# A two-layer mixing network followed by a transformer block, on one core: queue orders changed in the index, scan, attention and mixing stages

## The reference

```python
h = rms_norm(x, norm1_g[l]) * (1.0 + sc1) + sh1
proj = h @ w_in[l]
q, k, v, iq, ik, iw, z, xbc, dt_raw, ga, gm = jnp.split(proj, SPLIT_POINTS, axis=-1)
# q, k: normed and rotated; iq, ik: rotated
score = einsum("bqh,bqhs->bqs", iw, relu(einsum("bqhd,bsd->bqhs", iq, ik))) * IDX_SCALE
# 64 best keys of each query, softmax attention over them
o_attn = dsa_attention(q, k, v, iq, ik, iw, n_keep) @ w_attn_o[l]
xbc = silu(causal_dwconv(xbc, ssm_conv_w[l], ssm_conv_b[l]))   # 4 taps
y = ssd_scan(xs * dt_g, a_dt, bm, cm)       # decay = exp(cs[t] - cs[s]), s <= t, 32 heads
y = rms_norm((y + xs * d_skip) * silu(z), ssm_norm_g[l])       # by 4 groups
o_ssm = y @ w_ssm_o[l]
mixed = (sigmoid(ga) * o_attn + sigmoid(gm) * o_ssm) @ w_out[l]
x = x + g1 * mixed
h = rms_norm(x, norm2_g[l]) * (1.0 + sc2) + sh2
val, gate = jnp.split(causal_dwconv(h @ w_up[l], ffn_conv_w[l], ffn_conv_b[l]), 2, axis=-1)
x = x + g2 * ((silu(gate) * val) @ w_down[l])
```

## Time and profile before

| | |
|---|---|
| median of 3 runs | 1947.29 us (1946.86 to 1948.07) |
| profiled execution | 1950.46 us, span of its instructions 1948.8 us |
| PE busy | 1725.1 us, 89% of the span |
| POOL, DVE, ACT busy | 1165.8, 1005.3, 863.5 us |
| mean granted TensorE clock | 0.924 of full |
| read from HBM | 299.5 MB, 154 GB/s over the span |

### The profile page before, as it was taken

One profiled execution on the slowest core, in us unless ns is written; L12 is line 12 of the kernel. 1 busy time (PEld: TensorE's weight loads), 2 busy tenths in 40 slices (PEclk: granted clock), 3 DMA queues, 4 the chain that ended last, 5 costly groups with the idle time before them and its releaser, 6 DMA issues.

```text
span 1948.8 us, 33455 instructions
## 1 busy us (share of the span) xinstructions
PE 1725.1 (89%) x13290; PEld 1660.3 (85%) x13290; DVE 1005.3 (52%) x1772; ACT 863.5 (44%) x1411; POOL 1165.8 (60%) x476
## 2 busy tenths in 40 slices
PE   8978998979888999778999888888999895769999
PEld 8978988869888999778988778887999894669999
DVE  3457666456325886557666536424882247334400
ACT  2244444544335663244444454334664442324532
POOL 1346954545365889456865454455888683036886
PEclk8788999989899999888999998899999998578999
DMA  7334743436343558444754355444665652024664
GB/s 261 101 115 152 251 139 130 141 130 225 109 143 126 184 196 286 132 120 135 246 175 137 119 163 163 153 129 119 183 185 179 209 174 87 1 80 137 184 184 131
DMA packets 85513, 302.71 MB, mean 155 GB/s; under 512 B 9840, under 2 KB 12528, under 8 KB 85104
## 3 DMA queue, kind: packets, MB, share of 16 engines
q1 hardware_dynamic: 85360, 300.59, 48.3%
HBM read 299.50 MB, written 1.05 MB: 154 GB/s over the span
## 4 chain that ended last, share of the span: by engine, by line
PE 71%; DVE 15%; ACT 4%; issue 4%; DVEq 3%; DMA 1%; POOL 1%; SPq 0%; ACTq 0%; POOLq 0%
PE gemm_bank L1426 58%; PE turn_bank L1533 2%; DVE ada_acc L735 2%; ACT w_hi L404 2%; PE turn_bank L1503 1%; DVE conv L735 1%; PE outp_bank L1521 1%; PE score_bank L1426 1%; PE score_bank L1503 1%; DMA ada_w<-in_w_ada 1%; POOL w_lo L386 1%; DVE rstd_row L755 1%; DVE idx_score L735 1%; DVE probs L922 1%; PE outp_bank L1568 1%
## 5 line engine op out<-in xcount | busy, mean ns | idle before, releaser
L386 POOL TENSOR_TENSOR w_lo<-w_raw,w_hi 128x1024 fp32r<-128x1024 f32 x472 | 1165.6, 2476 | 771.4 <-ACT w_hi L404 770.9
L404 ACT ACTIVATE w_hi<-w_raw 128x1024 fp32r<-128x1024 f32 x472 | 492.3, 1046 | 767.2 <-PE gemm_bank L1426 738.0
L1426 PE MATMUL gemm_bank<-h_hi,w_hi 128*128 128x256 f32 x2112 | 617.8, 293 | 79.2 <-DVE h_lo L735 28.9
L1426 PE MATMUL gemm_bank<-h_lo,w_hi 128*128 128x256 f32 x2112 | 609.2, 288 | 0.0
L1426 PE MATMUL gemm_bank<-h_hi,w_lo 128*128 128x256 f32 x2112 | 608.6, 288 | 0.0
L1426 PEld LDWEIGHTS gemm_bank<-h_hi,w_hi 128*128 128x128 f32 x2112 | 417.8, 198 | 88.2 <-DVE h_lo L735 30.1
L1426 PEld LDWEIGHTS gemm_bank<-h_lo,w_hi 128*128 128x128 f32 x2112 | 417.8, 198 | 0.1
L1426 PEld LDWEIGHTS gemm_bank<-h_hi,w_lo 128*128 128x128 f32 x2112 | 417.2, 198 | 0.0
L1426 PE MATMUL gemm_bank<-w_hi,h_hi 128*128 128x256 f32 (+2 forms) x704 | 207.2, 294 | 18.4 <-DVE h_lo L735 8.0
L735 DVE SCALAR_TENSOR_TENSOR conv<-gemm_bank,params_sb,conv 128x255 f32<-128x255 f32 (+1 forms) x320 | 139.5, 477 | 140.7 <-ACT conv L567 69.8
L1426 PE MATMUL gemm_bank<-w_lo,h_hi 128*128 128x256 f32 (+2 forms) x704 | 202.7, 288 | 0.0
(11 more groups left out here) (276 smaller groups left out, 2407.4 us busy)
## 6 DMA issues: line engine op xcount, KB each, us to landing
w_raw<-in_stream SPq DMA_DIRECT2D x458, 512.0 KB, 3.6
ada_w<-in_w_ada SPq DMA_DIRECT2D x80, 512.0 KB, 4.7
ada_first<-in_w_ada SPq DMA_DIRECT2D x16, 512.0 KB, 10.5
w_raw<-in_stream SPq DMA_DIRECT2D x8, 256.0 KB, 2.7
alibi_sb<-in_alibi SPq DMA_DIRECT2D x1, 1920.0 KB, 7.2
rows_sb<-in_rows SPq DMA_DIRECT2D x1, 1536.0 KB, 10.5
residual<-in_x_t SPq DMA_DIRECT2D x1, 1024.0 KB, 7.4
out_x<-residual SPq DMA_DIRECT2D x4, 256.0 KB, 4.4
```

What stands on the lines that cost most here:

```text
L386: nc.gpsimd.tensor_tensor(w_lo[:, s, 0:n], w_raw[:, s, 0:n], w_hi[:, s, 0:n].bitcast(f32), ALU.subtract).then_inc(lo_ready, 1)
L404: A(w_hi[:, s, 0:n], w_raw[:, s, 0:n], ACT.Copy).then_inc(hi_ready, 1)
L1426: ins = M(o, a, b, start=first and i == 0, stop=last and i == len(passes) - 1, skip_group_check=True)
```

## The change

It does these things, in both layers if nothing else is said.

1. Index turns: DVE copies rounds 0 and 1 right behind the taps of unit 0, ahead of the softplus, and round 2 behind the taps of unit 1.
2. Index scores: ACT takes relu in place in PSUM and signals `relu_done`; DVE reads the bank and gives it back (`S.read`). The buffer `idx_relu` is no longer used.
3. Exponents: `pick` and `cs_split` have 128 rows in place of 64, the new ones zero.
4. Scan order on PE: the chunk of head h ahead of the exponents of head h+1.
5. End of the scan: on ACT the roots of the second half two parts into the tail rather than behind it; on DVE the low parts of the first half ahead of the scales of the second.
6. Last attention pair: `so_part(14)` ahead of the pair's values and transposes.
7. Mixing on ACT: the high parts between the weight copies of `U_AO` rather than behind them.
8. Modulation tiles of layer 0: eight in the up stage, on every other unit, and eight in the down stage, in place of sixteen there.

```diff
-        cs_split = sb("cs_split", [64, SEQ], f32r)
-        pick = sb("pick", [64, 32], f32r)
+        cs_split = sb("cs_split", [P, SEQ], f32r)
+        pick = sb("pick", [P, 32], f32r)
...
             if l + 1 < DEPTH:
-                slots += [((U_DN + i // 4, i % 4), ada_tile(l, "down", i)) for i in range(16)]
+                slots += [((U_UP + 2 * i + 2, 0), ada_tile(l, "down", i)) for i in range(8)]
+                slots += [((U_DN + i // 3, 2 * (i % 3)), ada_tile(l, "down", 8 + i)) for i in range(8)]
...
                             act.wait_ge(S.full[b], k + 1)
-                            if h >= 2:
-                                act.wait_ge(relu_used, l * IDX_HEADS + h - 1)
-                            A(idx_relu[:, h % 2, :], S.bank[b][:, 0:CW], ACT.Relu).then_inc(S.read[b], 1)
+                            A(S.bank[b][:, 0:CW], S.bank[b][:, 0:CW], ACT.Relu).then_inc(relu_done, 1)
...
-                late_parts(tail_parts(0, 5))
+                late_parts(tail_parts(0, 2))
                 y_roots(1)
+                late_parts(tail_parts(2, 5))
                 y_high(l, 0)
...
-                ahead(l, crossed(U_AO) + parts(U_AO + 2, U_OUT))
-                for j in range(4):
+                def mix_high(j):
                     act.wait_ge(mix_ready, l * 4 + j + 1)
                     A(HH[:, 2 * j:2 * j + 2, :], gates[:, 0, 2 * j:2 * j + 2, :], ACT.Copy, scale=0.5).then_inc(mix_hi, 1)
+                ahead(l, crossed(U_AO) + [(U_AO + 2, 0)])
+                mix_high(0)
+                mix_high(1)
+                ahead(l, [(U_AO + 2, 1), (U_AO + 3, 0)])
+                mix_high(2)
+                ahead(l, [(U_AO + 3, 1)])
+                mix_high(3)
...
-            V.tensor_tensor(pick[:], ident[0:64, 0:32], ident[0:64, 32:64], ALU.add)
+            V.tensor_tensor(pick[:], ident[:, 0:32], ident[:, 32:64], ALU.add)
+            V.tensor_scalar(cs_split[64:P, 0:P], ident[64:P, :], 0.0, None, ALU.mult)
+            V.tensor_scalar(cs_split[64:P, P:SEQ], ident[64:P, :], 0.0, None, ALU.mult)
...
                         b, k = S.use(l, S_IDX + h)
-                        dve.wait_ge(S.read[b], k + 1)
+                        dve.wait_ge(relu_done, l * IDX_HEADS + h + 1)
...
-                                ins = stt(idx_score[:, a:e], idx_relu[:, h % 2, a:e], iw[:, tt, h:h + 1], idx_score[:, a:e],
+                                ins = stt(idx_score[:, a:e], S.bank[b][:, a:e], iw[:, tt, h:h + 1], idx_score[:, a:e],
                                           ALU.mult, ALU.add)
-                        ins.then_inc(relu_used, 1)
+                        ins.then_inc(S.read[b], 1)
...
                     conv_taps(i)
+                    if i < 2:
+                        idx_turned((0, 1) if i == 0 else (2,))
                     if i == 0:
...
-                    elif i == 1:
-                        idx_turned()
                     elif 3 <= i < 7:
                         idx_scores(i - 3)
...
+                for f in range(8):
+                    y_low(f)
                 for f in range(8, 16):
                     y_scale(f)
-                for f in range(8):
-                    y_low(f)
...
                         up_low(i - 2)
+                    if l + 1 < DEPTH and i % 2 == 0 and 2 <= i < 18:
+                        ada(ada_tile(l, "down", i // 2 - 1))
...
-                        for i in range(4 * j, 4 * j + 4):
-                            ada(ada_tile(l, "down", i))
+                        for i in range(3 * j, min(3 * j + 3, 8)):
+                            ada(ada_tile(l, "down", 8 + i))
...
-                    if l < DEPTH and p < 7:
+                    if l < DEPTH:
                         so_part(2 * p)
...
                 if l < DEPTH:
-                    so_part(14)
                     so_part(15)
...
-                    row = pick[:, h:h + 1].to_broadcast([64, P])
+                    row = pick[:, h:h + 1].to_broadcast([P, P])
...
                 for h in range(16):
+                    part(l, *scan_part(h), token_chunk, HH, HL)
                     decay_exponents(h + 1)
-                    part(l, *scan_part(h), token_chunk, HH, HL)
...
                 for h in range(16, 32):
+                    late_part(*scan_part(h))
                     if h < 31:
                         decay_exponents(h + 1)
-                    late_part(*scan_part(h))
```

More of the change, by code:

```diff
@@ L254, in build @@
             sem("sq_ready"), sem("x_root"), sem("h_scaled"), sem("h_hi_ready"), sem("h_ready"))
-        idx_rot, relu_used = sem("idx_rot"), sem("relu_used")
+        idx_rot, relu_done = sem("idx_rot"), sem("relu_done")
         qk_squared, qk_sum, qk_root, q_rot, k_rot = sem("qk_squared"), sem("qk_sum"), sem("qk_root"), sem("q_rot"), sem("k_rot")
@@ L1038, in conv_taps, with idx_turned @@
                     ins.then_inc(gemm_read[b], 1)
-                def idx_turned():
-                    for r in range(3):
+                def idx_turned(rounds):
+                    for r in rounds:
                         b, k = T.use(l, T_IQ + r)
@@ L1049, in idx_scores @@
                         b, k = S.use(l, S_IDX + h)
-                        dve.wait_ge(S.read[b], k + 1)
+                        dve.wait_ge(relu_done, l * IDX_HEADS + h + 1)
                         for a, e, tt in ((0, P, 0), (P, CW, 1)):
                             if h == 0:
-                                ins = V.tensor_scalar(idx_score[:, a:e], idx_relu[:, 0, a:e], iw[:, tt, 0:1], None, ALU.mult)
+                                ins = V.tensor_scalar(idx_score[:, a:e], S.bank[b][:, a:e], iw[:, tt, 0:1], None, ALU.mult)
                             else:
-                                ins = stt(idx_score[:, a:e], idx_relu[:, h % 2, a:e], iw[:, tt, h:h + 1], idx_score[:, a:e],
+                                ins = stt(idx_score[:, a:e], S.bank[b][:, a:e], iw[:, tt, h:h + 1], idx_score[:, a:e],
                                           ALU.mult, ALU.add)
-                        ins.then_inc(relu_used, 1)
+                        ins.then_inc(S.read[b], 1)
                         dve.drain()
```

## The result

Before 1947.68 us (median of four runs, 1946.86 to 1949.45), changed 1928.18 us (four runs, 1925.02 to 1931.36), ratio 0.9905 with a 95% interval of 0.9885 to 0.9924. The profiled execution took 1931.36 us, its span is 1929.7 us; before it was 1948.8. Two of the four executions took 1931.3 us and two 1925.0, at a mean granted clock of 0.916 and 0.921, and the profiled one is of the longer pair. The change is faster, by 19.5 us where 55 were forecast.

A forecast was written before the change was run, and what follows sets the result against it. It took the kernel as bound by PE (71% of the chain; DVE 15%), with PE's waits for DVE left to win. Gains of 77.4 less 22 give 55.4, so a median of 1892 us; 8-in-10 range 1866 to 1924.

The forecast's parts named there:

- index stage: Turned queries copied earlier, score banks handed back by DVE: new PE stops and restarts, a loss of 11 per layer, -22 us.
- end of the scan: Root earlier on ACT, scales behind the first eight subtractions on DVE: 10.5 us saved per layer, +21.
- exponents: In the scan, 128 rows in place of 64 save 0.2 us for each of 62 heads, +12.4 us.
- order in the scan: Chunk ahead of the next head's exponents, so PE no longer waits there for DVE's `probs`: +9 us.
- last pair and mixing: Two terms: `so_part(14)` moved into PE's wait for `probsT`, +13 us; ACT's high parts made earlier at the mixing, +15.
- modulation tiles: Eight of layer 0's tiles moved into the up stage, relieving the down stage: +7 us.
- DVE's list up to the `ikT` copy is as long as before: Index stage: `ikT` is ready at 109.1 plus some 0.4 for the copy, leaving PE a wait of 5.2 us.
- 9.4 us leave the path: Scan's end: the root comes at about 407 and the scales stand behind eight subtractions, shortening DVE's chain by 9.4 us.
- a modulation tile sits between: Scan: where a tile (1.3 us or more) precedes the pair product, its exponents are late; 4 us given back.
- POOL holds up DVE: Rival, 14%: DVE waits for POOL at the scan's end, mixing, up-stage tiles and scan gates; 22 us (6 + 5 + 5 + 6) lost, 1914.
- The half clock throughout the index stage: Rival, 17%: the clock stays low between index stops of 6.2 us, 25 us more in two layers, 1917.
- The hand-over is free: Rival, 4%: the scores come early enough after all, 33.4 us shrinks to 7.6 per layer, 1840.

The follow-up runs named there:

- experiment 3: The changed kernel with the exponents over 64 rows again and no zero rows: 1940.52 us, 12.3 slower than the changed kernel.
- experiment 7: The changed kernel with the scan's end as before (root behind all five late chunks, scalings ahead of the low parts): 1938.67 us, 10.5 slower than the changed kernel.
- experiment 8: The changed kernel with the last attention pair and the mixing back in the old order: 1946.36 us, 18.2 slower than the changed kernel.
- experiment 4: The changed kernel with all sixteen modulation tiles in the down stage of layer 0 again: 1932.67 us, 4.5 slower, not clear of noise.
- experiment 5: The changed kernel with POOL's subtraction cut to 8 columns at thirteen chunks per layer: 1897.84 us, 30 us less than the changed kernel.
- experiment 10: The changed kernel with only heads 0 to 15 of the scan back in the old order: 1945.57 us, 17.4 slower than the changed kernel.
- experiment 6: The changed kernel with only heads 16 to 31 of the scan back in the old order: 1918.63 us, 9.6 us less than the changed kernel.
- experiment 2: The changed kernel with DVE's scores one unit earlier, relu still in PSUM: 1876.14 us, 52 us less than the changed kernel.

## Why the prediction was wrong

Faster was right; 1928.2 lies above the range of 1866 to 1924. By the landmarks the terms come to some 16.5 us in place of 55.4; the start and the end of the program make up the rest of the 19.1 between the two profiles. Of the 39 that are missing 15.5 belong to the index stage, which by itself put the time outside the range, and about 8 each to the end of the scan and to the last pair with the mixing.

| term | forecast | measured | by |
|---|---|---|---|
| index stage | -22 | -37.5 | landmarks |
| exponents | +12.4 | +12.3 | experiment 3 |
| order in the scan | +9 | +6 | both halves +18.5, less the exponents |
| end of the scan | +21 | +10.5 to 12.9 | experiment 7, landmarks |
| last pair and mixing | +28 | +18 to 20 | experiment 8, landmarks |
| modulation tiles | +7 | +2.7 to 4.5, not clear of noise | landmarks, experiment 4 |

*Index stage.* The mechanism was right, and its sign: six stops of 6.5 to 6.9 where 6.2 were forecast. The step that failed is "DVE's list up to the `ikT` copy is as long as before". It has the same instructions, but 3.7 us more. PE no longer stands still during softplus, so POOL goes on, and four of its steps are held up where two were; the stop was 8.6 for 5.2, and 1.7 at most in experiment 5. Nor did the sum hold the stop for `c_dot_b`, 2.8 per layer where it was 0.6, and 1.4 behind it (7.16 us for the next pair of chunks). By the rows it comes from DVE's running sum meeting POOL (scan and cast 2.4 us each, where before they took 0.7 and 0.3); no run takes these subtractions away. With 1.2 for the three longer stops, and 0.4 less of restarts, this is the 7.8 per layer.

*End of the scan.* "9.4 us leave the path" took the reciprocal and its steps at the durations of the earlier trace rows and left out that POOL stood still there only because PE did. Moved ahead of the stop, they run beside it and take 5.6 us more; experiment 7 shows the same steps short, experiment 5 shows them short in the new place without POOL. There the stage is 2.7 us shorter, in each layer, and ACT's high part, which the prediction named as next, sets the stop of 2.6 that is left. So POOL took 2.7 of the 4 us per layer that are missing. In the rest is PE's new wait of 1.0 to 1.2 us at the modulation sum; no run separates it.

*Exponents.* That 12.3 met 12.4 is in part luck: the price was 0.28 per head and not 0.2, and 5 us of it were hidden. Experiment 10 shows that the gain exists only in the new order.

*Scan.* The size of +9 was near, for a wrong reason. In layer 0 the first half, to the eighth pair product, gains 10.0 us and the second loses 0.7; in layer 1 they gain 7.0 and 2.2. In the second half "a modulation tile sits between" was not the trouble, but that the new order gathers two stops into one of 7.8, behind which more work runs at the low level (experiment 6). Undoing that half alone gains 9.6.

*Mixing and last pair.* Of the forecast 7.5 and 6.5 per layer 6.0 and 5.4 came in layer 0: 1.75 of stop is left at the mixing, and it is two subtractions held up; in experiment 5 the stop is gone and the stage 3.5 us shorter. In layer 1 the stage of the last pair gained only 2.8. The stops in it are no longer than in experiment 10, where it gained 7.2: the 4.4 between them is work at the low level (mean granted clock 0.91 for 0.99). What brings the clock down there stays open.

*Tiles.* "DVE has 25 us to give" was right, but each tile's sum except the first took 3.25 us or more beside POOL and PE waited 0.75 seven times.

*The rivals.* "POOL holds up DVE" was what happened, given 14%, and sized too small: 22 us at four places. Experiment 5, which leaves the tiles of the up stage alone, found 30, and in its trace half of the gain lies in the index stage, at softplus, which was not among the four. The half clock throughout the index stage did not come: restarts cost 9.2 of the forecast 9.6 per layer. "The hand-over is free" did not come either, but experiment 2 shows that it was one line away. The pair product did not wait in every pair.

*The signs named.* `idx_score` six times and some 37: 39.3. `ikT` twice and 10: 17.5, wrong. The line of 27.5 to fall to 6 to 8: 10.7. The mixing's stops to vanish: 1.75 each. `probs` near 3: the stops in front of the exponents went, and 23.5 stands at the pair product instead. Up and down stage within 6 us of layer 1: 189.4 us against the 178.8 of the earlier trace rows, wrong.

## What to carry to other kernels

A duration read from a stretch in which GpSimd stands still doesn't hold for the same instruction moved into a busy stretch: here 0.2 to 0.7 us became 2.1 to 2.9, and work of 9.4 us that was pulled out of a stop took 5.6 us more in its new place, 2.7 of them on PE's path. It also holds for work that isn't moved: end a stop of PE, and POOL goes on beside what stayed (softplus). When a resource is handed back by another engine than before, lay the two queues side by side and ask what stands ahead of the hand-back; one unit's shift was worth 52 us. In the second half of the scan one stop of 7.8 us cost more than two of 1.9 and 2.6, by 9.6 us in two layers, partly through the work at the low clock behind it.

## What was not expected of the hardware

- Operations with one SBUF input are held up as well: TENSOR_SCALAR 2.49 us for 0.43, CAST 2.42 for 0.28, and a TENSOR_SCALAR on 64 columns 1.46 for 0.19. The reciprocal over 512 columns lasts 3.35 us beside POOL (at 330.55) and without it (at 417.18 before the change).
- In the first half of the scan a chunk took 2.93 us behind waits of 0.9 to 1.0 us (experiment 10) and 2.94 behind one of 1.67 (before the change), but 4.22 behind one of 1.76 (experiment 10). In the second half it took 4.11 behind one of 1.9 and 2.92 behind one of 2.6 that came 7.6 us later (experiment 6). The length of the stop alone doesn't tell whether the low level follows.
- A head's exponents are four matmuls, two of them on `cs_split`. With these two over 64 rows the group cost 0.28 us more between chunks over 128 rows than with all four over 128, though the columns are the same.
